# Seven half-sized products for some weight groups of three feed-forwards, with their evictions in stages

## The reference

```python
def swiglu(h, w_in, w_out):
    gu = h @ w_in                       # 512x1024 @ 1024x5632
    a, b = gu[..., :D_FF], gu[..., D_FF:]
    return (jax.nn.silu(a) * b) @ w_out # D_FF = 2816

for l in range(DEPTH):                  # DEPTH = 2
    x = x + 0.5 * swiglu(rmsnorm(x, norm_ffn1[l]), w_ffn1_in[l], w_ffn1_out[l])
    h = rmsnorm(x, norm_mix[l])
    x = x + mixing_sublayer(h, ...)
    x = x + 0.5 * swiglu(rmsnorm(x, norm_ffn2[l]), w_ffn2_in[l], w_ffn2_out[l])
```

## Time and profile before

| | us |
|---|---|
| runs of the kernel: median (lowest to highest) | 3125.64 (3125.53 to 3126.32) |
| the profiled execution: span from first to last instruction | 3124.5 |
| TensorE matmul busy in it | 3108.5 (99%) |
| VectorE busy | 1536.1 (49%) |
| ScalarE busy | 1097.2 (35%) |
| GpSimd busy | 253.3 (8%) |

### The profile page before, as it was taken

How to read it: one execution, slowest core, us unless ns; L and a number is a source line. 1 busy time by engine, 2 the same in 40 slices (tenths; PEclk the granted TensorE clock), 3 DMA queues, 4 the chain that set the end, 5 groups by cost and what they waited for, 6 DMA issues and landing times.

```text
span 3124.5 us, 35882 instructions
## 1 busy us (share of the span) xinstructions
PE 3108.5 (99%) x14334; PEld 2531.9 (81%) x14334; DVE 1536.1 (49%) x2472; ACT 1097.2 (35%) x1536; POOL 253.3 (8%) x223
## 2 busy tenths in 40 slices
PE   9999999999999999999999999999999999999998
PEld 7888887788888888888877788888888877888887
DVE  6434436565443444344456555434556555564352
ACT  5323335333322332233344333322456433332222
POOL 0000104102000010000022011000201000110001
PEclk9999999999999999999999999999999999999999
DMA  5333322222433233333222233233332333333332
GB/s 155 95 96 97 131 88 68 75 81 95 140 96 96 91 105 95 101 95 115 95 75 68 69 105 110 95 95 97 105 107 78 97 96 100 101 95 95 101 94 74
DMA packets 95044, 302.01 MB, mean 97 GB/s; under 512 B 11088, under 2 KB 21456, under 8 KB 94300
## 3 DMA queue, kind: packets, MB, share of 16 engines
q1 hardware_dynamic: 94880, 299.73, 30.8%
HBM read 297.54 MB, written 5.29 MB: 97 GB/s over the span
## 4 chain that ended last, share of the span: by engine, by line
PE 99%; DMA 0%; DVE 0%; ACT 0%; issue 0%; SPq 0%; POOL 0%; POOLq 0%; ACTq 0%; DVEq 0%
PE bank L1657 93%; PE score_ps L1483 1%; PE out_ps L1516 1%; PE turn_ps L1494 1%; PE out_ps L1535 1%; PE score_ps L1525 1%; PE score_ps L1557 1%; PE score_ps L1607 0%; PE turn_ps L1503 0%; PE out_ps L1568 0%; PE turn_ps L1432 0%; PE turn_ps L1414 0%; DMA raw<-w_ffn_in 0%; PE out_ps L1595 0%; PE score_ps L1585 0%; DMA rgw<-rg_in 0%
## 5 line engine op out<-in xcount | busy, mean ns | idle before, releaser
L2075 DVE TENSOR_TENSOR w_lo<-raw,w_hi 128x1024 fp32r<-128x1024 f32 (+1 forms) x548 | 674.5, 1231 | 1188.1 <-ACT w_hi L1689 1187.6
L1657 PE MATMUL bank<-in_hi,w_hi 128*128 128x512 f32 x2704 | 1077.5, 398 | 1.0 <-DVE in_lo L2081 1.0
L1657 PE MATMUL bank<-in_hi,w_lo 128*128 128x512 f32 x2704 | 1054.4, 390 | 0.0
L1657 PE MATMUL bank<-in_lo,w_hi 128*128 128x512 f32 x2704 | 1053.7, 390 | 0.0
L1689 ACT ACTIVATE w_hi<-raw 128x1024 fp32r<-128x1024 f32 (+1 forms) x548 | 567.3, 1037 | 1095.7 <-PE bank L1657 1089.0
L1657 PEld LDWEIGHTS bank<-in_hi,w_hi 128*128 128x128 f32 x2704 | 507.9, 188 | 125.5 <-issue 20.9
L1657 PEld LDWEIGHTS bank<-in_hi,w_lo 128*128 128x128 f32 x2704 | 507.5, 188 | 108.2
L1657 PEld LDWEIGHTS bank<-in_lo,w_hi 128*128 128x128 f32 x2704 | 508.2, 188 | 103.5 <-issue 2.4
L1657 PE MATMUL bank<-hid_hi,w_hi 128*128 128x512 f32 x960 | 373.4, 389 | 0.0
L1657 PE MATMUL bank<-hid_lo,w_hi 128*128 128x512 f32 x960 | 373.4, 389 | 0.0
L1657 PE MATMUL bank<-hid_hi,w_lo 128*128 128x512 f32 x960 | 373.4, 389 | 0.0
(11 more groups left out here) (339 smaller groups left out, 2590.0 us busy)
## 6 DMA issues: line engine op xcount, KB each, us to landing
raw<-w_ffn_in SPq DMA_DIRECT2D x175, 512.0 KB, 3.5
raw<-w_mix SPq DMA_DIRECT2D x90, 512.0 KB, 3.5
raw<-w_ffn_out SPq DMA_DIRECT2D x80, 512.0 KB, 3.5
raw<-w_mixb SPq DMA_DIRECT2D x58, 512.0 KB, 3.6
raw<-w_mlp_in SPq DMA_DIRECT2D x32, 512.0 KB, 3.5
raw<-w_mlp_out SPq DMA_DIRECT2D x32, 512.0 KB, 3.5
raw<-w_w_out SPq DMA_DIRECT2D x16, 512.0 KB, 3.5
raw<-w_ffn_out SPq DMA_DIRECT2D x16, 256.0 KB, 2.7
```

Source lines behind the costliest of these rows:

```text
L1657: mm = pe.matmul(ps, lhs, rhs, start=first and step == 0, stop=last and step == 2, skip_group_check=True)
L2075: dve.tensor_tensor(w_lo[:, i % SPLIT, cut], raw[:, i % RAW, cut], w_hi[:, i % SPLIT, cut].bitcast(F32), ALU.subtract).then_inc(S_["lo_spl ...
```

## The change

In three feed-forwards (ffn2 of layer 0, ffn1 and ffn2 of layer 1) 7 of the 22 groups of two output tiles are computed otherwise: the third, fourth and fifth silu group of the first piece, and the first four of the second. The 2 output tiles, 2 halves of 4 input blocks and 2 halves of 256 tokens form 2x2 blocks, and seven products of blocks (12 matmuls of 128x256 each, L2047) with sums before and after stand in place of eight. Four beats hold them: S1 and S2 of two products, S3 of one, S4 of two. S3 and S4 come after the first and after the second unit of the plain hidden group that follows.

- The sums of input blocks ("forms") are made once per feed-forward: 8 scaled copies on ScalarE, 4 sums on VectorE, 4 splits in halves on both.
- The sums of weight blocks, t1 to t4, are made on VectorE for each group, in place in `raw`, before the split. Seven products need 7 x 512 columns of split weights in place of 4 x 512.
- Products are added up partly in PSUM: between two of them ScalarE copies 256 columns out (m1, u2, u3, c21), and VectorE combines them with another bank (c11, c22, c12). Three banks are used, `sums`, `plain` and `apart`.
- `finish_silu` then multiplies both tiles (128 x 1024) by the norm's factor, and one ScalarE instruction applies silu to both.
- Evictions of the plain groups near them go in stages a beat apart (`later`): `evict_hidden`, then the high halves, then the low halves. A hidden group is not evicted before its silu group is through (`awaiting`).
- PSUM banks come from a free list (`Banks`), which has 7 in these stages. Each bank carries the semaphore value that frees it. Plain groups take with `low=True`, which sorts banks 0 to 3 first.
- Four more buffers of raw weights (`raw_more`); the mlp goes in three pieces (12, 10, 10) because 12 hidden tiles have room now; the memory of the second block is loaded and prepared later, during the last products out of ffn2 of layer 1; the decay table is loaded once per layer.

```diff
-HID = 16
+HID = 12
+QUARTER = UNIT // 2
+LEFT, RIGHT = slice(0, S // 2), slice(S // 2, S)
+MORE_RAW = 4
+PLAIN_FIRST = {"ffn1_in0": (12, 10), "ffn2_in0": (4, 0), "ffn1_in1": (4, 0), "ffn2_in1": (4, 0), "mlp_in": (6, 5, 5)}
...
+def by_products(name, piece, n_groups):
+    return [PLAIN_FIRST[name][piece] <= i < n_groups - 2 and i % 2 == 0 for i in range(n_groups)]
...
+class Banks:
+    def take(self, n, low=False):
+        if low:
+            self.free = deque(sorted(self.free, key=lambda b: b >= 4))
+        return tuple(self.free.popleft() for _ in range(n))
+    def __setitem__(self, banks, over):
+        for b in banks:
+            self.over[b] = over
+            self.free.append(b)
...
                 if k0 == 0:
-                    beat["bank_over"] = self.bank_over[g % 2]
+                    banks = self.bank_over.take(2, True)
+                    beat["bank_over"] = self.bank_over.overs(banks)
...
+    def seven_products(self, name, out, finish):
+        sums = self.bank_over.take(1)
+        plain = self.bank_over.take(1)
+        self.weight_sums(st, self.beats[-2], "t1", "t2")
...
+        self.product_beat([piece(0, first, 0, None, UNIT)],
+                          [product("left_first", 0, sums, True), product("left_last", QUARTER, plain, True)])
+        def after_first(units=self.units()):
+            self.copy_out(st, "m1", units, sums[0], 0, LEFT)
+            self.combine(st, "c11", units, plain[0], 0, LEFT, "m1", "add")
+            self.bank_over[plain] = ("st_combined", st["c11"])
...
+        self.weight_sums(st, self.beats[-1], "t3", "t4")
+        apart = self.bank_over.take(1)
+        self.product_beat([piece(0, first, 0, "t1"), piece(QUARTER, "t2", 0, "t2")],
+                          [product("difference", 0, apart, True), product("second", QUARTER, sums, False, "m1")])
...
+        def third():
+            self.product_beat([piece(0, second, 0, "t3")], [product("third", 0, sums, False, "u2")])
...
+        def fourth():
+            self.product_beat([piece(0, first, QUARTER, "t4"), piece(QUARTER, second, QUARTER, None)],
+                              [product("right_last", 0, sums, False, "u3"), product("fourth", QUARTER, apart, False, "c22")])
+            def after_fourth(units=self.units()):
+                self.copy_out(st, "c21", units, sums[0], 0, RIGHT)
+                self.combine(st, "c12", units, apart[0], 1, LEFT, "u2", "subtract")
+                self.later.append(lambda: finish(st))
...
-                it = self.item("evict_hidden", units=units, pair=pair, gated=gated, parts=[],
+                if outs[0][0] - n_hidden in awaiting:
+                    self.later.append(lambda: evict_in(outs, units, pair, first, held, awaiting, apart))
+                    return
+                it = self.item("evict_hidden", units=units, pair=pair, gated=gated, parts=[], apart=apart,
...
                 self.bank_over[pair] = ("dve_evict", part["v"])
...
+            def products(b):
+                pe.wait_ge(S_["lo_split"], i + 1)
+                for part in b["products"]:
+                    for name, value in part["over"]:
+                        pe.wait_ge(S_[name], value)
+                    for which in part["waits"]:
+                        pe.wait_ge(S_["st_combined" if which == "c22" else "st_copied"], part["st"][which])
+                    ps = bank[part["bank"]][:, 0:S // 2]
+                    for k in range(TT):
+                        for step, (x, y) in enumerate(((hi, wh), (lo, wh), (hi, wl))):
+                            mm = pe.matmul(ps, y, x, start=part["start"] and k == 0 and step == 0,
+                                           stop=k == TT - 1 and step == 2, skip_group_check=True)
...
+                elif kind == "finish_silu":
+                    pair = out_pair(it["st"]["out"])
+                    dve.tensor_tensor(pair, pair, rstd_twice, ALU.mult).then_inc(S_["dve_evict"], 1)
```

More of the change, by code:

```diff
@@ L156, in __init__ @@
         self.cursor = {}
-        self.bank_over = [None, None]
+        self.bank_over = Banks(4)
+        self.loads, self.left, self.many_banks, self.later = [], deque(), False, []
         self.into = self.prologue
@@ L243, in gemm @@
                         self.into = items = []
-                        evict([((tiles[0], o), o) for o in range(2)], ("half_used", beat["half"]), 1 - g % 2)
+                        evict([((tiles[0], o), o) for o in range(2)], ("half_used", beat["half"]), others)
                         beat["slots"].append((at_, items))
@@ new lines, in product_beat @@
+    def product_beat(self, pieces, products):
+        i = self.units()
+        beat = dict(i=i, early=[], slots=[], tail=[], pieces=pieces, products=products, load=None, half=None)
+        self.beats.append(beat)
+        self.inp.through = i + 1
+        self.into = beat["tail"]
+        self.flush()
+        self.item("split_hi", i=i + AHEAD)
+        self.item("split_lo", i=i + AHEAD)
+        beat["split_end"] = len(beat["tail"])
+        if self.hooks:
+            self.hooks.popleft()()
+        for fn in self.timed.pop(i, ()):
+            fn()
+        self.run_later()
+        return beat
@@ new lines, in run_later, with copy_out, combine @@
+    def run_later(self):
+        todo, self.later = self.later, []
+        for fn in todo:
+            fn()
+    def copy_out(self, st, which, units, bank, tile, half):
+        st[which] = self.add("st_copied")
+        self.item("st_copy", st=st, which=which, units=units, bank=bank, tile=tile, half=half)
+    def combine(self, st, which, units, bank, tile, half, copied, op):
+        st[which] = self.add("st_combined")
+        self.item("st_combine", st=st, which=which, units=units, bank=bank, tile=tile, half=half, copied=copied, op=op)
@@ L419, in feed_forward, with evict @@
             self.hid_open = self.hid.through
             self.hid.ready = {}
-            self.gemm(w_in, DT, swiglu_groups(first, n) if gated else pairs(first, n), self.inp, evict_in)
+            groups = swiglu_groups(first, n) if gated else pairs(first, n)
+            seven = by_products(w_in, piece, len(groups))
+            if any(seven) and not made:
+                made = True
+                self.make_forms()
+            for i, (tiles, by_seven) in enumerate(zip(groups, seven)):
+                if not by_seven:
+                    apart = any(seven) and i < len(groups) - 1
+                    def evict(outs, units, pair, apart=apart):
+                        if apart:
+                            self.later.append(lambda: evict_in(outs, units, pair, apart=True))
+                        else:
+                            evict_in(outs, units, pair)
+                    self.gemm(w_in, DT, [tiles], self.inp, evict, fresh=tiles is groups[0])
+                    continue
+                j = tiles[0]
+                in_silu = gated and j < n_hidden or not gated and (j // 2) % 2
+                ring = "silu" if in_silu else "tmp"
+                places = (self.silu if in_silu else self.tmp).take_pair()
+                out = dict(ring=ring, b=places[0].b, places=places)
+                if gated and j < n_hidden:
+                    held[j], held[j + 1] = places
+                    awaiting.add(j)
+                    self.seven_products(w_in, out, lambda st, j=j: finish_silu(st, j))
+                else:
+                    self.seven_products(w_in, out, lambda st, j=j: finish_hidden(st, j))
@@ L2572, in starts, with in_pieces @@
     return [[first_col + t * P for t in g] for g in groups]
+def in_pieces(name, groups):
+    out = []
+    for piece, g in enumerate(groups):
+        out.append((0, DT, [tuple(c) if seven else c for c, seven in zip(starts(0, g), by_products(name, piece, len(g)))]))
+    return out
 def plans():
```

471 lines of the change are left out of this document (397 added, 74 removed).

## The result

| | before | after |
|---|---|---|
| runs: median (lowest to highest), us | 3125.65 (3125.53 to 3126.32) | 3161.61 (3159.87 to 3162.91) |
| span of the profiled execution, us | 3124.5 | 3161.1 |
| mean granted clock of TensorE over it | 0.998 | 0.994 |

The ratio is 1.0114, 95% interval 1.0102 to 1.0127: 36 us slower. The forecast of 3149.4 had the sign, the place and the mechanism of the wait; it lies 12 us low. The profiled execution is the longest of the four; their spans run from 3158.1 to 3161.1 us.

The account below looks back on a forecast made before the run. TensorE bounds the kernel, busy 3108.5 of 3124.5 us. 3124.5 - 16.8 (matmuls removed) + 36.9 + 3.7 (waits) = 3148.3 span, plus 1.1 for the median: 3149.4 us; own range 3144 to 3168, 8-in-10 range 3132 to 3170.

Parts of the forecast that it names:

- What is removed: TensorE matmuls in 21 silu groups: 10.08 us by products against 10.88 plain, 0.80 a group, 16.8 us gained.
- the 25 us estimated above: Gain over all product groups by the Trainium skill's per-matmul formula, 1.19 us a group; the trace's pace was used instead.
- The wait: TensorE's first plain unit after S2 (or S1) waits for VectorE's eviction: 15 of 2.46 us, 3 of 1.24; 36.9 plus 3.7.
- Forecast walk: VectorE's queue from S1's start to the second hidden tile's eviction, ending 8.08 us; TensorE starts at 8.22 instead of 5.76.
- Other waits and hidden work: Copies, splits, c22, sums, forms, mlp pieces and memory preparation taken as covered, at 0; c22 up to 0 to 4 us.
- The clock: TensorE's clock was taken to stay full through the new gaps, as at a 1.67 us gap; 0 in the sum.
- rival 2: TensorE's clock falls in the gaps, about 2.2 us each, 15 of them: +33, 3182 us; chance 0.05.
- slower `finish_silu`: The 1024-wide VectorE operation might take 2.1 us instead of 1.14, making the wait 3.4 us.
- late `c22`: The combination S4's second product needs, ready at 8.3 us, needed at 8.32: up to 0.4 us in 9 places.
- Rival 1: VectorE's queue before the second eviction is under 5.76 us, so no wait forms: 3108.8 us; chance 0.09.

Follow-up runs that it names:

- e1: The change, but plain groups in stages with products take the PSUM banks free longest, not banks 0 to 3 first; 3110.16 us, 0.9949 of before.
- e5: The change with no group by products in any feed-forward, its side changes kept; 3126.69 us, 1.0003 of before.
- e8: The kernel before, with TensorE waiting at 15 units for VectorE's low half of the weights two units on; 3180.41 us, 1.0175 of before.
- e6: The change with weight sums t3, t4 and the split of S3's weights moved behind the hidden group's evictions on VectorE; 3122.67 us, 0.9990 of before.
- e9: The kernel before, with TensorE waiting at 15 units for ScalarE's high half of the weights two units on; 3148.80 us, 1.0074 of before.
- e2: The change with the hidden group's evictions ahead of the split of S3's weights in S2's tail; 3157.30 us, 1.0099 of before.
- e3: The change with two idle 128-wide subtractions on VectorE ahead of the low split of S3's weights; 3169.24 us, 1.0138 of before.
- e4: The change with four idle 128-wide subtractions on VectorE ahead of the low split of S3's weights; 3195.51 us, 1.0224 of before.

## Why the forecast was right in the mechanism and 12 us low

- **What is removed.** Forecast 0.80 us a group at 0.2267 and 0.120 us a matmul, 16.8; measured 0.755 a group, 15.9 (e1). Right, not the eighth that seven for eight promises. By the Trainium skill's formula ("TensorE: Matmul & The Clock Gate", Back-to-back issue gap) it would have been the 25 us estimated above; e1 measured 15.9, and the measurement decides.
- **The wait.** Forecast walk: low split 1.63, t3 2.77, t4 3.38, finish 3.99, c11 5.13, split 5.46, evict 6.07, product 6.79, evict 7.40, TensorE 8.22. Measured, from the start of S1 at 833.91: 1.57, 2.71, 3.31, 3.91, 5.05, 5.38, 5.98, 6.70, 7.31, TensorE 8.05. Every operation is 0.06 to 0.09 earlier than forecast, and TensorE starts 0.06 behind VectorE's end and not 0.14. Forecast 15 waits of 2.46 and 3 of 1.24; measured 2.12 + 0.27 = 2.39 and 0.93 + 0.27 = 1.20, at the places named. `finish_silu`, whose cost no row of before bounded well, took 1.22, with the next operation 1.14 behind its start, as taken.
- **Other waits and hidden work, at nothing.** Right: no gap before any S beat, and e5 puts the side changes at 0.
- **The clock, the step that failed.** The forecast took the clock to stay at full through the gaps because it had at one gap of 1.67 us, called the fall "unlikely" and priced it at 0 in the sum. One row was read as a rule. That gap keeps full clock in all these traces too, yet of gaps of 1.75, in another kernel, 8 in 15 brought a fall. Neither side of rival 2 was right: falls come behind 7 of the 15 gaps, not all, and cost 1.6 and not 2.2 each. The term is 11 us in place of 0 or 33. The Trainium skill's warning on gaps between bursts ("TensorE: Matmul & The Clock Gate", Why this matters for your kernels) holds here, by e8 without any other cause, and already for gaps shorter than those that it names.
- **Outside the sum.** About 1.5 us at the start, where this execution waited 2.19 us for VectorE's `in_lo` and had a clock fall at 13 us. In the other kernels' traces the start-up lies between 0.9 us earlier and level with before, with the same instructions, so this varies with the execution. In the memory, 0.9 longer in its keys and 0.5 shorter in the fifth piece leave 0.4 more.
- **The range.** That 3161.6 lies inside it is in part luck: its upper side was meant for a slower `finish_silu` and a late `c22`, and neither came. The clock, priced at 0, filled that room; 15 falls would have left it.

Sum by measured terms: -15.9 + 35.9 + 3.6 + 11.2 + 1.5 + 0.4 = 36.7 us, against 36.6 measured in spans. The forecast had -16.8 + 36.9 + 3.7 = 23.8; of the difference of 12.8, 11.2 is the clock.

The better version is e1: 0.5% faster than before and 1.6% faster than the change. Rival 1's figure for "no wait", 3108.8, is within 1.4 us of it.

The 0.045 us that each group saves less than forecast are the switches of width, nearly all of them. In e1 the first five steps of a plain unit behind products take 1.16 us (836.07 to 837.23) where five at the pace take 1.13, twice a group; the first steps of S1 and S3 give 0.01 back.

What stays open: why a gap of one length brings a fall at one place and not at the next, with rows that look alike ahead of it.

## What to carry to other kernels

A change that removes work from the engine that is the bound can create its first wait, and then the wait is set by another engine's queue, less what the engine itself still has to do meanwhile, whatever the other's average load (VectorE 53% here): walk the queue from the head to the operation that frees the buffer, and look first at whether another free buffer would do (here one argument gave back 51 us). Price each such gap as the view's number, plus drain and slow first steps (0.27 us here), plus the chance of half clock behind it. Compare matmul counts in equal windows: a lowered clock shows as busy time, not as a wait.

## What the runs showed of the hardware

- TensorE's clock behind a single gap between dense stretches at full clock, by shown length of the gap, in one execution of each kernel:

| gap, us | 0.55 | 0.93 | 1.25 | 1.75 | 2.12 | 2.51 | 2.66 | 3.31 |
|---|---|---|---|---|---|---|---|---|
| kernel | e6 | four | e9 | e2 | the change | e8 | e3 | e4 |
| falls to half | 0 of 15 | 0 of 12 | 0 of 15 | 8 of 15 | 7 of 15 | 5 of 15 | 9 of 15 | 14 of 15 |

 e8's column holds its gaps of 2.79 (no fall) and 4.07 (fall), e9's its gaps of 1.53 and 1.03. Between 1.75 and 2.66 us the counts differ by no more than the spans of several executions of one kernel allow, so no order among them is shown; none at up to 1.25 and nearly all at 3.31 stand out. In the change the fall comes between 0.2 us before and 0.8 after the matmuls start again, so nearly all of it is paid by them; in e4 up to 1.4 us of it lie in the gap.
- The first step between matmuls after a stop is longer at full clock too: 0.33 us where the pace is 0.227.
- The first five steps of 512 columns behind products of 256 take 1.16 us in place of 1.13 (e1).
- 21 groups of 84 matmuls of 256 columns, each with a weight load of its own, held 0.12 us each with VectorE, ScalarE and DMA at work beside them (e1), as in the memory keys.
